# Eleven weight slots instead of nine for the experts of a two-layer mixture-of-experts trunk

## The reference, cut to what matters

```python
x = layer_norm(ALPHA * x + g1 * out, P['ln_w'][l, 0], P['ln_b'][l, 0])
h = x * (1.0 + sc2) + sh2
y = moe_ffn(h, P['router_w'], P['router_bias'], P['moe_w_gate'][l], P['moe_w_up'][l], P['moe_w_down'][l])
x = layer_norm(ALPHA * x + g2 * y, P['ln_w'][l, 1], P['ln_b'][l, 1])
# moe_ffn: scores = sigmoid(t @ router_w); top 2 experts of the best group; comb = their weights
hg = jnp.einsum('td,edf->tef', t, w_gate)     # w_gate, w_up: 16 x 1024 x 512 per layer
hu = jnp.einsum('td,edf->tef', t, w_up)
act = jax.nn.silu(hg) * hu * comb[:, :, None]
y = jnp.einsum('tef,efd->td', act, w_down)    # w_down: 16 x 512 x 1024 per layer
```

## Time and profile before

| | |
|---|---|
| time, median of 3 runs (lowest to highest) | 1278.73 us (1278.3 to 1278.73) |
| profiled execution, its own time | 1281.8 us |
| its span | 1280.1 us |
| mean granted TensorE clock | 0.907 |
| TensorE matmuls busy | 1009.5 us (79%) |
| VectorE, ScalarE, GpSimd busy | 416.9, 229.7, 192.8 us |
| moved from and to DRAM | 344.59 MB, 269 GB/s over the span |
| chain that ended last: TensorE, DMA, VectorE | 60%, 20%, 11% |

### The profile page before, as it was taken

The page is one execution under the profiler, slowest core; times in us unless marked ns, Lnnn a source line. Parts: engine busy times, 40 slices in busy tenths (PEclk is TensorE's granted clock), DMA queues, the critical chain, the costliest instruction groups (busy, mean ns, idle before and its releaser), DMA issues.

```text
span 1280.1 us, 24187 instructions
## 1 busy us (share of the span) xinstructions
PE 1009.5 (79%) x9506; PEld 572.9 (45%) x9506; DVE 416.9 (33%) x1139; ACT 229.7 (18%) x459; POOL 192.8 (15%) x382
## 2 busy tenths in 40 slices
PE   0899999789699777796389998988979997775930
PEld 0444447554555444453245554445465553342510
DVE  0220015864612221122553234553542221111207
ACT  0401002431412111111221111110322121110202
POOL 1200000200122221222210000001022221211231
PEclk9999999899689998899689998999959998987975
DMA  9985332967479999999994211444631969999973
GB/s 317 383 277 197 131 139 91 352 246 307 173 278 389 393 402 411 393 396 369 393 378 145 92 66 48 182 197 148 251 160 42 378 236 401 395 398 413 396 274 131
DMA packets 79819, 344.59 MB, mean 269 GB/s; under 512 B 9158, under 2 KB 9609, under 8 KB 67468
## 3 DMA queue, kind: packets, MB, share of 16 engines
q1 hardware_dynamic: 57108, 289.30, 58.4%
q0 software_dynamic: 14608, 43.35, 9.7%
q10 hardware_dynamic: 8040, 11.01, 2.5%
HBM read 320.01 MB, written 23.63 MB: 268 GB/s over the span
## 4 chain that ended last, share of the span: by engine, by line
PE 60%; DMA 20%; DVE 11%; SPq 3%; ACT 3%; issue 2%; POOL 0%; POOLq 0%; DVEq 0%; ACTq 0%; PEldq 0%
PE bank L856 15%; DMA ring<-in_moe_w_up_dram 15%; PE bank L646 11%; PE bank L921 10%; PE bank L772 6%; PE bank L863 6%; DMA ring<-in_ada_w_dram 3%; SPq L1351 3%; PE bank L833 2%; DMA ring<-in_moe_w_down_dram 1%; PE bank L599 1%; PE bank L995 1%; PE bank L1019 1%; ACT arena L1204 1%; DVE arena L1320 1%
## 5 line engine op out<-in xcount | busy, mean ns | idle before, releaser
L856 PE MATMUL bank<-ring,arena 128*32 128x256 f32 x3072 | 193.5, 409 | 50.6 <-DMA ring<-in_moe_w_up_dram 50.6
L856 PEld LDWEIGHTS bank<-ring,arena 128*32 128x32 f32 x3072 | 104.9, 118 | 132.6 <-issue 78.2
L646 PE MATMUL bank<-ring,hT 128*128 128x512 f32 x336 | 144.9, 593 | 1.0 <-ACT hT L1055 1.0
L1318 DVE TENSOR_TENSOR arena<-arena,bank 128x64 f32<-128x64 f32 x136 | 27.4, 202 | 317.0 <-ACT arena L1204 317.0
L921 PE MATMUL bank<-hT,ring 128*128 128x384 f32 x384 | 124.6, 487 | 1.0 <-ACT hT L1055 1.0
L863 PE MATMUL bank<-ring,arena 128*32 128x256 f32 x1536 | 92.8, 382 | 27.3 <-DVE arena L1320 25.4
L599 PE MATMUL bank<-ring,small 128*32 128x256 f32 x768 | 53.8, 443 | 58.7 <-DMA ring<-in_ada_w_dram 58.7
L646 PEld LDWEIGHTS bank<-ring,hT 128*128 128x128 f32 x336 | 63.7, 190 | 80.4 <-issue 79.2
L921 PEld LDWEIGHTS bank<-hT,ring 128*128 128x128 f32 x384 | 72.9, 190 | 52.3 <-ACT hT L1055 1.2
L856 PE MATMUL bank<-arena 128*32 128x256 f32 x1216 | 72.8, 393 | 13.9 <-DMA arena<-in_moe_w_up_dram 13.9
L533 POOL DMA_DIRECT2D arena<-slot_rows x140 | 70.8, 506 | 59.6 <-POOL arena L543 42.8
(11 more groups left out here) (325 smaller groups left out, 1112.6 us busy)
## 6 DMA issues: line engine op xcount, KB each, us to landing
ring<-in_ada_w_dram SPq DMA_DIRECT2D x24, 2048.0 KB, 19.6
ring<-in_moe_w_gate_dram SPq DMA_DIRECT2D x22, 2048.0 KB, 21.9
ring<-in_moe_w_up_dram SPq DMA_DIRECT2D x22, 2048.0 KB, 27.2
ring<-in_moe_w_down_dram SPq DMA_DIRECT2D x22, 2048.0 KB, 30.1
arena<-in_moe_w_gate_dram SPq DMA_DIRECT2D x10, 2048.0 KB, 35.1
arena<-in_moe_w_up_dram SPq DMA_DIRECT2D x10, 2048.0 KB, 40.6
arena<-in_moe_w_down_dram SPq DMA_DIRECT2D x10, 2048.0 KB, 43.9
ring<-in_ev_w_in_dram SPq DMA_DIRECT2D x7, 2048.0 KB, 15.6
```

The lines of the kernel that those rows point to most:

```text
L646: last = pe.matmul(bank[3 * (c % 2) + t], hT[:, k, t * P:(t + 1) * P], slot8(n)[:, k, :], start=k == 0, stop=k == KT - 1)
L856: last = pe.matmul(bank[1][q * BLK:(q + 1) * BLK, 0:HALF], slot_inT[:, k, :], both[:, :, k, q * P:(q + 1) * P], start=k == 0, stop=k == KT ...
L1318: dve.tensor_tensor(act_rows[:, two, :], silu_g[:, two, :], up, ALU.mult).then_inc(S["gated"], 1)
```

## The change

`MOE_RING` becomes 11. The experts' slots are no longer dealt out in threes: gate and up of place p take pair number p % 4 of (0,1), (3,4), (6,7), (9,10), and the down matrix takes slot 2, 5 or 8 by p % 3. The two new slots 9 and 10 are the first 8192 columns of one tensor `whole` that now holds `hT` (in its first 4096 columns) and `arena` behind it: slot 9 lies over `hT`, slot 10 over `h_tok`. The block buffers move from column 3072 of the arena to 19456, and the arena grows by 1024 columns. Two semaphores are saved by letting `zero_rdy` and `idle_set` share `pool_chain`, and `slot_row_in` share `ck_in`. The slots of `BETWEEN` are dealt anew.

```diff
-MOE_RING = 9
+MOE_RING = 11
+PAIR_SLOTS = [(0, 1), (3, 4), (6, 7), (9, 10)]
+DOWN_SLOTS = [2, 5, 8]
 CHUNK = 4096
+HT_ROOM = CHUNK
...
-    slots = [(i + 2) % STAGING for i in range(len(BEFORE))] + [i % MOE_RING for i in range(3 * NE)]
-    slots += [(i + 3) % STAGING for i in range(len(BETWEEN) - 6)] + [0, 1, 2, 0, 3, 4] + [i % MOE_RING for i in range(3 * NE)]
+    experts = [slot for place in range(NE)
+               for slot in (*PAIR_SLOTS[place % len(PAIR_SLOTS)], DOWN_SLOTS[place % len(DOWN_SLOTS)])]
+    slots = [(i + 2) % STAGING for i in range(len(BEFORE))] + experts
+    slots += [0, 1, 3, 4, 2, 0, 1, 3, 4, 2, 0, 1, 3, 4, 2, 0, 3, 4] + experts
...
-        hT = sb("hT", [P, KT, T])
-        arena = sb("arena", [P, 19456])
+        whole = sb("arena", [P, HT_ROOM + 20480])
+        hT = whole[:, 0:KT * T].rearrange("p (k t) -> p k t", t=T)
+        arena = whole[:, HT_ROOM:HT_ROOM + 20480]
...
-        slot_in = at(3072, 512, rows=2 * BLK)
-        slot_inT = at(3584, KT, BLK)
-        silu_g = at(3840, FT, BLK)
-        act_rows = at(3968, FT, BLK)
+        slot_in = at(19456, 512, rows=2 * BLK)
+        slot_inT = at(19968, KT, BLK)
+        silu_g = at(20224, FT, BLK)
+        act_rows = at(20352, FT, BLK)
...
             s = SLOT[n]
+            if s >= 9:
+                return whole[:, (s - 9) * CHUNK:(s - 8) * CHUNK]
             return ring[:, s, :] if s < RING else at(SPARE + (s - RING) * CHUNK, CHUNK)
...
-            dve.wait_ge(slot_row_in, 16)
+            dve.wait_ge(ck_in, 32)
...
-                def next_expert(place, group):
-                    e = sp.value_load(order[0:1, bass.ds(place, 1)], min_val=FIRST, max_val=NE - 1)
+                for place in range(FIRST, NE):
+                    e = sp.value_load(order[0:1, place:place + 1], min_val=FIRST, max_val=NE - 1)
                     for j in range(3):
-                        if j != 1:
-                            expert_through(layer, place - 3, j)
-                        expert_matrix(sp, layer, e, first + 3 * group, j)
-
-                with sp.Fori(1, NE // 3) as three:
-                    for group in range(3):
-                        next_expert(three * 3 + group, group)
-                next_expert(NE - 1, 0)
+                        if j == 2:
+                            expert_through(layer, place - len(DOWN_SLOTS), 2)
+                        elif place == len(PAIR_SLOTS) - 1:
+                            if j == 0:
+                                sp.wait_ge(htok_mm, 6 * (layer + 1))
+                            else:
+                                sp.wait_ge(scattered, 16 * 6 * (layer + 1))
+                                sp.wait_ge(pick_mm, layer + 1)
+                                sp.wait_ge(MS[layer]["row_in0"], 32)
+                        elif j == 0:
+                            expert_through(layer, place - len(PAIR_SLOTS), 0)
+                        expert_matrix(sp, layer, e, first + 3 * place, j)
...
-            pool.memset(zeros, 0.0).then_inc(zero_rdy, 1)
-            pool.wait_ge(zero_rdy, 1)
+            pool.memset(zeros, 0.0).then_inc(pool_chain, 1)
+            pool.wait_ge(pool_chain, 1)
...
-    nc = _bacc.Bacc("TRN2", target_bir_lowering=False, num_devices=1)
+    nc = _bacc.Bacc("TRN2", target_bir_lowering=False, num_devices=1, dynamic_dma_scratch_size=8192)
```

More of the change, by code:

```diff
@@ L384, in trunk_program @@
         rlog_mm, rscore, htok_mm, htok_act = [sem(n) for n in ("rlog_mm", "rscore", "htok_mm", "htok_act")]
-        mask_rdy, pos_mm, table_rdy, idx_rdy, zero_rdy, trips_rdy, order_rdy, zeroed, scattered, ln_first = [sem(n) for n in (
-            "mask_ready", "pos_mm", "table_ready", "idx_ready", "zero_ready", "trips_ready", "order_ready", "zeroed", "scattered", "rows_scaled")]
-        pick_rdy, pick_mm, slot_row_in = sem("pick_ready"), sem("pick_mm"), sem("slot_row_in")
+        mask_rdy, pos_mm, table_rdy, idx_rdy, trips_rdy, order_rdy, zeroed, scattered, ln_first = [sem(n) for n in (
+            "mask_ready", "pos_mm", "table_ready", "idx_ready", "trips_ready", "order_ready", "zeroed", "scattered", "rows_scaled")]
+        pick_rdy, pick_mm = sem("pick_ready"), sem("pick_mm")
         MS = [{n: sem(f"{n}_{layer}") for n in (
@@ L400, in trunk_program @@
         out_done = sem("out_done")
-        idle_set = sem("idle_set")
+        pool_chain = sem("pool_chain")
         router_in = sem("router_in")
@@ L449, in pair_of @@
             s = SLOT[n]
-            two = ring[:, s:s + 2, :].rearrange("p w c -> p (w c)") if s < RING else at(SPARE + (s - RING) * CHUNK, 2 * CHUNK)
+            two = whole[:, 0:2 * CHUNK] if s == 9 else ring[:, s:s + 2, :].rearrange("p w c -> p (w c)") if s < RING else at(SPARE + (s - RING) * CHUNK, 2 * CHUNK)
             return two.rearrange("p (w k n) -> p w k n", w=2, k=KT)
@@ L548, in pool_moe @@
             pool.wait_ge(S["down_mm"], before_last)
-            pool.tensor_tensor(idle, wsel[:, 0, 0:1], wsel[:, 0, 0:1], ALU.add).then_inc(idle_set, 1)
-            pool.wait_ge(idle_set, 2 * l + 1)
+            pool.tensor_tensor(idle, wsel[:, 0, 0:1], wsel[:, 0, 0:1], ALU.add).then_inc(pool_chain, 1)
+            pool.wait_ge(pool_chain, 2 * l + 2)
             ln_rows(pool, 2 * l + 1)
@@ L556, in pool_moe @@
             pool.wait_ge(S["rowT"], blocks + 1)
-            pool.tensor_tensor(idle, wsel[:, 0, 0:1], wsel[:, 0, 0:1], ALU.add).then_inc(idle_set, 1)
-            pool.wait_ge(idle_set, 2 * l + 2)
+            pool.tensor_tensor(idle, wsel[:, 0, 0:1], wsel[:, 0, 0:1], ALU.add).then_inc(pool_chain, 1)
+            pool.wait_ge(pool_chain, 2 * l + 3)
             for t in range(NT):
@@ L1436, in gpsimd_program @@
             pool.wait_ge(ret_dve, NT)
[L1437 removed]
+            pool.dma_start(slot_row, a["c_keep"][:, K_SLOT:K_ALL]).then_inc(ck_in, 16)
             pool.wait_ge(out_done, 16 * OUT_DMAS)
```

## The result

| | before | after |
|---|---|---|
| time, median | 1278.73 us | 1268.70 us |
| lowest to highest, 5 runs each | 1278.3 to 1284.09 | 1261.9 to 1273.05 |
| profiled execution, its own time | 1281.8 us | 1272.33 us |
| its span | 1280.1 us | 1270.6 us |
| mean granted TensorE clock of it | 0.907 | 0.908 |

The medians differ by 10.0 us. The ratio after to before, formed from the runs and not from the two medians, is 0.9911, with a 95% interval of 0.9885 to 0.9938. Two later comparisons of the same two kernels gave 0.9932 (0.9908 to 0.9956) and 0.9899 (0.9866 to 0.9932), with medians of 1269.74 against 1278.86 and 1268.80 against 1278.78. The forecast was 1259, 19.4 us faster. The direction was right, and the time lies in the stated range of 1254 to 1271, but only half of the forecast gain came.

The account below looks back on a forecast made before the run. The prediction took full DMA engines to bound the expert stages, so only their idle time could be won: 9.7 us per layer, 19.4 us in all, from 1278.7 to 1259 us, range 1254 to 1271.

Parts of the forecast that it names:

- The sum: Whole kernel: 9.7 us from each layer, 19.4 us together, from a median of 1278.7 to 1259.3 us.
- What bounds the kernel: Expert stages: DMA engines are full near 400 GB/s, so more slots win only time in which they now stand idle.
- Layer 0, the start: First experts of layer 0: gate 3 at about 349.2 us, up 3 at 364.5, the stream 8.2 us ahead.
- Layer 0, the middle: Layer 0 near 575 to 580 us: the queue no longer runs dry before gate 15, worth 1.5 us.
- After the experts of layer 0: Chunks, layer norm and gathers after layer 0's experts: all move with the stream, carrying over all 9.7 us.
- The Hyena stage only moves: Hyena stage between the layers: it is TensorE's own and only starts earlier, near 646 us instead of 655.
- Layer 1: Layer 1's experts: up 6 lands at 1067.0 us instead of 1076.71, and the 9.7 us lead stays to the last expert.
- The edits at nothing: Whole kernel: moved block buffers, shared semaphores and SP's unrolled loop cost nothing, the loop a few tenths of a us at most.
- Half comes back: Rival, chance 0.15: only one layer's lead survives, layer 0's perhaps lost on the way to 650 us; 1269 us.
- It does not do what it says: Rival, chance 0.05: gate 3 and up 3 are still held to the first block's end; 1.5 to 3 us, 1276 us.
- the halved scratch: Rival, chance 0.04: halving the descriptor scratch makes the kernel slower.
- More than the bounds: Rival, chance 0.07: TensorE's clock falls after stalls, so fewer stalls win a few us more; 1253 us.

Follow-up runs that it names:

- repeat: The changed kernel run again with no edit: 1269.74 us, ratio 0.9932 to the kernel before.
- repeat2: The changed kernel run once more with no edit, in a later comparison: 1268.80 us, ratio 0.9899 to the kernel before.
- l1_off: The changed kernel, but layer 1 has the gate waits of the kernel before: 1277.20 us, ratio 0.9990 to the kernel before.
- l1_no_start: The changed kernel, but in layer 1 gate 3 waits for place 0's gate/up products as before, later gates as changed: 1268.64 us, ratio 0.9907.
- l1_only_start: The changed kernel, but in layer 1 only gate 3 and up 3 go early, later gates wait for place p-3 as before: 1277.65 us, ratio 0.9978.
- scratch: The kernel before with only the descriptor scratch halved to 8192 bytes: 1278.11 us, ratio 0.9995.
- l0_off: The changed kernel, but layer 0 has the gate waits of the kernel before: 1271.43 us, ratio 0.9934 to the kernel before.
- hold: The changed kernel, but gate 3 too waits for the scatters: 1270.07 us, ratio 0.9922 to the kernel before.
- no_row: The changed kernel without up 3's wait for the first rows brought back: 1272.08 us, ratio 0.9932 to the kernel before.

## Why the prediction was right or wrong, point by point

**The sum.** The forecast was 9.7 us from each layer. Over the profiles, layer 0's expert stage gave 4.1 us and layer 1's 7.8 us, 11.9 together; the medians of the three comparisons differ by 10.0, 9.1 and 10.0 us. So most of what is missing, 5.6 us, is missing in layer 0. That the time lies inside the stated range is partly luck: the forecast's own bounds, 1256 to 1262.5, were missed, and the range reached 1271 only to hold a rival whose reason did not come true.

**What bounds the kernel: right.** The share of the DMA engines is still 1.01 through both expert stages, and the stalls for gate and up matrices went from 20.0 us (18.4 and 1.6 for slots in the arena) to 20.3 in layer 0 and from 44.4 us to 36.8 in layer 1, TensorE's waits from 366 to 598 us and from 968 to 1229 us in the kernel after:

```profile
PE bank L864 <- DMA ring<-in_moe_w_up_dram: 16.9, 3, 9.4
...
PE bank L864 <- DMA arena<-in_moe_w_up_dram: 3.4, 1, 3.4
```

```profile
PE bank L864 <- DMA ring<-in_moe_w_up_dram: 22.6, 3, 8.5
...
PE bank L864 <- DMA arena<-in_moe_w_up_dram: 14.2, 3, 8.4
```

In layer 0 the stalls did not shrink at all, although the last matrix landed 3 us sooner (595.5 instead of 598.5, forecast near 589). So the stalls' sum does not measure the lead: TensorE also ran for 17.3 us of that stage at half clock in this profile, against 23.5 before.

**Layer 0, the start: the failed step.** I took up 3's release at 364.5, between 362.1 and 366.8; it came at 368.04, outside these bounds. Six profiles have layer 0 as changed (after, repeat, repeat2, l1_off, l1_no_start, l1_only_start). Counted from the stage's first block (359.9 us in the kernel before), up 3 was to go out at 4.6 us; it went out at 7.1 to 8.4, 7.7 in the mean. Nearly all of this is the scatters: they end 4.6 us after the first block in the mean, against 0.6 us before it in before, scratch and l0_off. That is 5.2 us later, the whole transfer of gate 3, where I took half of it. The rows behind them cost what I took: in five of the six profiles the first pair lands in 2.0 to 2.6 us each. Only in the first profile one of them took 3.5 us, and gate 3 had landed before it was issued (at 358.9), so the reason of that is open.

The other half was lost after the release. I let up 3 land 7.4 us after its issue because it is alone, and down 3 one interval later, 13.0 us in all; it took 15.6 to 16.6 us, 16.0 in the mean. A row for it stood in the trace of before: there gate 3 and up 3 go out into idle engines, 0.4 us apart, and land 9.4 and 15.8 us after their issues, the second one 16.2 us after the first issue (line 459 in the kernel before, 365.5 to 366 us):

```profile
DMA to landing us min/median/max: 9.4/12.6/15.8
```

For layer 1 I used the third landing of this burst, 22.3 us, and here not the second. In the first profile after, the landing of up 3 and of down 3 after their issue:

```profile
DMA to landing us min/median/max: 9.0/9.0/9.0
```

```profile
DMA to landing us min/median/max: 15.3/15.3/15.3
```

Down 3 landed at 369.3 + 15.3 = 384.6, forecast 377.5, before 387.5: a lead of 2.9 us, and 2.9 us too in the means of the profiles (23.7 against 26.7 us after the first block). The forecast of 8.2 was not even what its own landings give: 377.5 is 10.0 us ahead of 387.5, and its bounds of 375.5 to 381 make it 12 to 6.5 us.

**Layer 0, the middle: right in kind.** The dip near 575 us is gone. Forecast 1.5 us, measured 1.6 (238.6 against 236.9 and 237.0 us), or 0.4 to 3.5 by which of the three profiles with layer 0 as before is taken. Over the profiles with the change in layer 0 untouched (after, repeat, repeat2, l1_off, l1_no_start, l1_only_start) the expert stage takes 236.8 us in the mean, over those without it (before, scratch, l0_off) 240.9: 4.1 us instead of 9.7.

**After the experts of layer 0: right.** The first eviction is at 618.20 instead of 621.30 and the gathers begin behind 606.48 instead of 609.53, so the 3 us are carried over in full:

```profile
618.20 0.38 ACT L589 ACTIVATE ring<-bank 128x256 f32<-128x256 f32 x1 [18.35 <-PE bank L611]
...
606.48 0.19 POOL L565 TENSOR_TENSOR small<-small 128x1 f32<-128x1 f32 x1 [13.33 <-DMA slot_rows<-arena]
```

TensorE's wait for the chunks is 30.4 us, as it was the earlier trace rows. The Hyena products start at 652.4 instead of 655.4, forecast near 646. "The Hyena stage only moves" is not refuted: the stage takes 224.8 us in the mean of the 11 profiles whose layer 0 has any part of the change, against 223.6 in before, scratch and l0_off. They have 2.9 us more at half clock, which by the 4.1 us for each 10 us above makes 1.2 us, and single executions differ by 5 us. Whether the change has a part in that clock is open. Why `l1_off` shows 1.7 us where its stage in layer 0 is 4 us shorter is only in part explained by this; within the intervals it stays open.

**Layer 1: right, for one reason too many.** Up 6 was forecast to land 22.3 us after the burst from idle; up 6 of the kernel after was issued at 1047.8 and landed 18.9 us later, at 1066.7, against 1067.0 forecast and 1076.7 before. That these agree to 0.3 us is partly luck: the burst began at 1045.76 and not at 1044.71, and took 20.9 us. TensorE's wait for the weights of place 6, 7.3 us before, is gone, as forecast. That profile's stage begins 1.6 us later than before's, so the lead is 11.6 us there; over the ten profiles with the whole change to later gates it is 9.7 us at up 6 (105.4 us after the stage's first block in the mean, against 115.1 in before, scratch, l1_off and l1_only_start), as forecast. At the end of the stage 7.8 us are left (268.4 against 276.2 us). I had said that from there on the lead stays. It shrinks by 2 us: from up 6 to down 15 the stream takes 158.7 us with the lead and 156.8 without. A reason that fits half of it, by my estimate: with the stream ahead by 10 us TensorE computes 1.6 more blocks of 6.35 us in that stretch, each moving four row DMAs of 64 KB, 0.66 us at 398 GB/s; that was not tested. And the words on gate 3 and up 3 in layer 1 credited them with a part; `l1_no_start` shows that they have none.

**The edits at nothing** show no clear cost: `scratch` 0.9995. Block buffers, semaphores and the unrolled loop were not tested by themselves. With the unrolled loop the page's instruction queue q14 has 16 packets and 0.13 MB instead of 14 and 0.11 MB, and SP issues gate and up 4 of layer 0 0.44 us apart (370.97 and 371.41 us), against 0.47 us before (371.59 and 372.06 us). The stages that have them without the new waits take 242.5 us in layer 0 (`l0_off`, against 239.5 and 240.7 in scratch and before) and 275.7 us in layer 1 (`l1_off`, against 277.3 and 276.9), so a cost of 1 or 2 us in layer 0 is not excluded.

**The rivals.** "Half comes back" is what the number looks like, 1268.7 against its 1269, but not for its reason: nothing came back between the experts of layer 0 and the Hyena stage. The gain of layer 0 was mostly never there, because its start was mis-sized, and layer 1's was a fifth smaller. "It does not do what it says" did not occur, nor did the halved scratch: `scratch` took 1278.11 us against 1278.86 us. "More than the bounds" did not occur either. Its premise is in the trace of before: TensorE stops for 7.3 us at 1069.9 us and for 9.3 us at 1219.8 us, and the granted clock is 0.50 from 1073 to 1083 us and from 1223.1 to 1233.1 us. But the stalls of layer 1 shrank only from 44.4 to 36.8 us, and the clock of that stage rose from 0.88 to 0.89. Rows too late did not stop a block in the changed kernel; in `no_row` they stopped the second one for 4.7 us. Small transfers slowed beside a weight also held up 3: the scatters ended 5.2 us later in the mean, and in `hold` the rows took 6.5 to 8.3 us instead of 2.1 to 2.3.

**A weight DMA beside the scatters.** The trace of before had none. With gate 3 issued among them, whose transfer takes 5.3 us at 398 GB/s, the scatters ended 4.4 us later in the first profile and 5.2 in the mean. Down 3 landed 23.7 us after the first block and not at the 17.6 of the forecast, 6.1 us late; the scatters' full delay is 2.8 us of that, 3.0 us came after up 3's release, and the rest is small.

## What to carry to other kernels

More room for prefetch was worth the idle time of the DMA engines that lay just before the wait that set the stream's pace, and nothing beyond the spread of the profiles for idle time before another idle stretch. Layer 1 took 276.9 us before, 269.5 with the early later gates alone (`l1_no_start`) and 274.8 with the front alone (`l1_only_start`): this lead arrived early at a full set of slots and ran into 20.7 us at a DMA share of 0.17. When a large load is pulled into a stretch with small transfers on which something waits, price the wait with the whole large load before them (5.2 us here, of the 5.3 of a matrix), and find out which of them it will run beside: in the changed kernel it was the scatters, in `hold` and `no_row` the rows. Take the landing of the next loads from a burst of the same shape in the trace, not from one load alone: the second of two loads into idle engines landed 16.2 us after the first issue, where I had 13.0. And where the clock moves single executions by more than the effect, compare stages over several profiles: here the Hyena stage ran from 221.6 to 227.0 us with the us at half clock, more than the 4.1 us of layer 0.

## What the runs showed of the hardware

The six scatters of layer 0, with one 2 MiB load issued among them, ended 5.2 us later than without it (means of six profiles and of three: 4.6 us after the stage's first block against 0.6 us before it).

The 64 KB row DMAs that took 2.1 to 2.3 us with idle engines took 6.5 to 8.3 us beside a single 2 MiB load (`hold`), as much as with a long queue of them (4.3 to 8.4 us). The first pair beside up 3 in `no_row` took 7.2 and 8.4 us.

The kernel before took 1278.11 us with `dynamic_dma_scratch_size=8192` and 1278.86 us without it (ratio 0.9995, 0.9978 to 1.0012); in both, queue q0 (software_dynamic) moved 43.35 MB and the issues of `rows_ahead` took 496/508/577 ns.

The changed kernel's 17 timed runs spread from 1260.52 to 1273.08 us. Over the 14 profiles 10.2 to 23.9 us at half clock in the Hyena stage went with 221.6 to 227.0 us, for the same instructions.
